# mLSTM states of a hybrid decoder step stored as 64+1 columns a head pair instead of 2 x (64+1), with the sample update's masked keys made by GpSimd

## What is computed

```
a    = einsum(q, k) * d_w                                  # scores with decay weights
num  = a @ v + inter_w * (q @ C)                           # "inter" part reads the state
den  = sum(a)  + inter_w * (q @ n)
h    = num / max(|den|, exp(-m_t))
C    = decay * C + einsum('s,sk,sv->kv', w_s, k, v)        # update
n    = decay * n + einsum('s,sk->k', w_s, k)
```

## Time and profile before

| | us |
|---|---|
| median of 3 runs (lowest to highest) | 2176.08 (2172.74 to 2176.18) |
| the profiled execution's own time | 2176.46 |
| its span on the core | 2174.6 |
| TensorE busy | 1987.2 (91%) |
| VectorE busy | 963.5 (44%) |
| ScalarE busy | 430.4 (20%) |
| GpSimd busy | 80.1 (4%) |

### The profile page before, as it was taken

How to read it: one execution, slowest core, us unless ns; L and a number is a source line. 1 busy time by engine, 2 the same in 40 slices (tenths; PEclk the granted TensorE clock), 3 DMA queues, 4 the chain that set the end, 5 groups by cost and what they waited for, 6 DMA issues and landing times.

```text
span 2174.6 us, 30150 instructions
## 1 busy us (share of the span) xinstructions
PE 1987.2 (91%) x13082; PEld 1868.7 (86%) x13082; DVE 963.5 (44%) x1661; ACT 430.4 (20%) x803; POOL 80.1 (4%) x71
## 2 busy tenths in 40 slices
PE   5998887999797698889987798999999999999997
PEld 5997657999787468878986498999999999999997
DVE  7323674565366346684233125333333333332344
ACT  2003671011220143131023302110001000000126
POOL 3000002000101200000000000000000000000000
PEclk9999999999777799999999999999999999999998
DMA  4314802110242784134130511111111111111112
GB/s 143 111 29 160 310 2 53 39 49 22 94 180 97 273 339 164 40 97 126 29 135 17 197 39 39 39 46 36 53 39 46 36 53 43 42 37 53 44 34 83
DMA packets 165878, 188.55 MB, mean 87 GB/s; under 512 B 15919, under 2 KB 153679, under 8 KB 161050
## 3 DMA queue, kind: packets, MB, share of 16 engines
q1 hardware_dynamic: 164250, 153.70, 21.7%
q10 hardware_dynamic: 1536, 33.56, 4.0%
HBM read 170.46 MB, written 50.33 MB: 102 GB/s over the span
## 4 chain that ended last, share of the span: by engine, by line
PE 82%; DVE 9%; ACT 4%; issue 2%; SPq 1%; DMA 1%; DVEq 0%; ACTq 0%
PE psum L253 64%; PE psum L2025 2%; PE psum L485 2%; PE psum L1697 1%; PE psum L1297 1%; DVE x_lo L291 1%; PE psum L1000 1%; PE psum L509 1%; SPq L1239 1%; PE psum L497 1%; PE psum L990 1%; ACT wide L579 1%; PE psum L1348 1%; ACT scratch L1718 1%; PE psum L1312 1%
## 5 line engine op out<-in xcount | busy, mean ns | idle before, releaser
L253 PE MATMUL psum<-x_lo,weights_hi 128*128 128x384 f32 (+1 forms) x2328 | 517.9, 330 | 0.0
L253 PE MATMUL psum<-x_hi,weights_hi 128*128 128x384 f32 (+1 forms) x2136 | 479.2, 332 | 34.6 <-DVE x_lo L291 24.3
L253 PE MATMUL psum<-x_hi,weights_lo 128*128 128x384 f32 (+1 forms) x2136 | 473.9, 330 | 0.0
L208 DVE CAST weights_hi<-weights_raw 128x1024 fp32r<-128x1024 f32 (+1 forms) x138 | 91.9, 666 | 731.6 <-PE psum L253 719.1
L253 PEld LDWEIGHTS psum<-x_hi,weights_hi 128*128 128x128 f32 x2136 | 368.3, 190 | 39.7 <-issue 27.1
L253 PEld LDWEIGHTS psum<-x_lo,weights_hi 128*128 128x128 f32 x2328 | 402.0, 190 | 0.0
L253 PEld LDWEIGHTS psum<-x_hi,weights_lo 128*128 128x128 f32 x2136 | 368.4, 189 | 0.0
L210 DVE TENSOR_TENSOR weights_lo<-weights_raw,weights_hi 128x1024 fp32r<-128x1024 f32 (+1 forms) x138 | 161.7, 1172 | 4.7
L1941 ACT ACTIVATE scratch<-scratch 128x1088 f32<-128x1088 f32 x22 | 24.5, 1116 | 419.9 <-DVE scratch L1955 419.9
L253 PE MATMUL psum<-hidden_hi,weights_hi 128*128 128x384 f32 (+1 forms) x432 | 95.2, 328 | 0.0
L253 PE MATMUL psum<-hidden_lo,weights_hi 128*128 128x384 f32 (+1 forms) x432 | 95.2, 328 | 0.0
(11 more groups left out here) (338 smaller groups left out, 2408.2 us busy)
## 6 DMA issues: line engine op xcount, KB each, us to landing
weights_raw<-in_w_in_dram SPq DMA_DIRECT2D x28, 512.0 KB, 3.7
work<-in_cache_win_k_dram SPq DMA_DIRECT2D x6, 2048.0 KB, 13.1
work<-in_cache_win_v_dram ACTq DMA_DIRECT2D x6, 2048.0 KB, 12.8
weights_raw<-in_w_gate_dram SPq DMA_DIRECT2D x22, 512.0 KB, 3.7
weights_raw<-in_w_up_dram SPq DMA_DIRECT2D x22, 512.0 KB, 3.7
weights_raw<-in_w_down_dram SPq DMA_DIRECT2D x24, 384.0 KB, 3.3
weights_work<-in_cache_mem_k_dram SPq DMA_DIRECT2D x8, 1024.0 KB, 5.1
work<-in_cache_mem_v_dram SPq DMA_DIRECT2D x8, 1024.0 KB, 10.7
```

The source lines that it names most:

```text
L208: nc.vector.tensor_copy(whi[:, w, 0:nk, :], raw[:, w, 0:nk, :]).then_inc(w_high, 1)
L253: mm = nc.tensor.matmul(PS[:, 3 * s + c, 0:n], w[:, slot, k0 + k], x[part][:, k0 + k, t0:t0 + n], start=(k == 0 and w is whi and part == 0 ...
```

## The change

The odd head's block moves from columns 65:130 to columns 0:65 of its rows, so a pair takes 65 columns on all 128 partitions and nothing in a state is zero padding.

- Inter products read on row groups: two products a pair, K = 64 rows each, with 65 columns moving; the even heads go to bank 6, the odd to bank 7. 8 products a chunk for 4, and 64 for 32 in the sample phase.
- Update products write on column groups: one product a head, 64 weight columns, 65 moving, to PSUM rows 0:64 or 64:128 of one bank; 8 products for 4. In the sample phase they use bank 6 or 7 and no longer bank 4, so the wait for `c_cat` goes.
- Decay is one instruction for two, the addition one for four, the n copies one for two.
- The sample states are not zeroed; the 16 loads become 8 of 128 KB without a wait, the 18 state stores become 9.
- The masked keys are made by GpSimd, after its q mask and kw of the sample chunk, instead of VectorE.

```diff
-        cst = cut(XN, ML0 + 3448, NP, 2 * V1W)
+        cst = cut(XN, ML0 + 3448, NP, V1W)
-        sample_c = cut(WRT, 0, DB, NP * 2 * V1W)
+        sample_c = cut(WRT, 0, DB, NP * V1W)
...
+        def state_update_tensor(pe, k, c, n, bank):
+            for h in range(H):
+                p, rows = h // 2, slice(HD * (h % 2), HD * (h % 2) + HD)
+                mm = nc.tensor.matmul(PS[rows, bank, p * V1W:(p + 1) * V1W], k[0:n, h * HD:(h + 1) * HD],
+                                      v1[0:n, c, h * V1W:(h + 1) * V1W], start=True, stop=True, tile_position=(0, HD * (h % 2)))
+            return mm
...
                 for p in range(NP):
-                    mm = nc.tensor.matmul(PS[:, 6 + p // 2, (p % 2) * 2 * V1W:(p % 2 + 1) * 2 * V1W], qk[:, p, c * P:(c + 1) * P],
-                                          cst[:, p, :], start=True, stop=True)
+                    for e in range(2):
+                        rows = slice(HD * e, HD * e + HD)
+                        mm = nc.tensor.matmul(PS[:, 6 + e, p * V1W:(p + 1) * V1W], qk[rows, p, c * P:(c + 1) * P],
+                                              cst[rows, p, :], start=True, stop=True, tile_position=(HD * e, 0))
...
-                for p in range(NP):
-                    mm = nc.tensor.matmul(PS[:, 6 + p // 2, (p % 2) * 2 * V1W:(p % 2 + 1) * 2 * V1W], kw[:, p * P:(p + 1) * P],
-                                          v1[:, c, p * 2 * V1W:(p + 1) * 2 * V1W], start=True, stop=True)
-                mm.then_inc(c_upd, 1)
+                state_update_tensor(pe, kw, c, P, 6).then_inc(c_upd, 1)
...
         def state_decay(state, c):
-            for e in range(2):
-                rows, cs = slice(HD * e, HD * e + HD), slice(V1W * e, V1W * e + V1W)
-                last = nc.vector.tensor_tensor(state[rows, :, cs], state[rows, :, cs],
-                                               dec[rows, :, c:c + 1].to_broadcast([HD, NP, V1W]), ALU.mult)
-            chains["dve"](last)
+            chains["dve"](nc.vector.tensor_tensor(state, state, dec[:, :, c:c + 1].to_broadcast([P, NP, V1W]), ALU.mult))
-        def state_add(state, banks, signal):
-            for e in range(2):
-                rows, cs = slice(HD * e, HD * e + HD), slice(V1W * e, V1W * e + V1W)
-                for a in range(2):
-                    upd = PS[rows, banks + a, 0:4 * V1W].rearrange("p (j d) -> p j d", j=2)
-                    last = nc.vector.tensor_tensor(state[rows, 2 * a:2 * a + 2, cs], upd[:, :, cs], state[rows, 2 * a:2 * a + 2, cs], ALU.add)
-            last.then_inc(signal, 1)
+        def state_add(state, bank, signal):
+            upd = PS[:, bank, 0:4 * V1W].rearrange("p (j d) -> p j d", j=NP)
+            nc.vector.tensor_tensor(state, upd, state, ALU.add).then_inc(signal, 1)
...
+        def masked_k_pool(pool):
+            pool.wait_ge(c_kw, NC + 1)
+            for b in range(DB):
+                if b >= 2:
+                    pool.wait_ge(su_ready, b - 1)
+                nc.gpsimd.tensor_scalar(kwm[0:NS, b % 2, :], kw[0:NS, :], batch_sel[0:NS, b:b + 1], None, ALU.mult).then_inc(kwm_ready, 1)
...
                 for b in range(DB):
-                    mm = nc.tensor.matmul(PS[0:NS, 6 + p // 2, (p % 2) * 2 * V1W:(p % 2 + 1) * 2 * V1W],
-                                          q_mask[:, b, p * NS:(p + 1) * NS], sc4[:, b, p, :], start=(b == 0), stop=(b == DB - 1))
+                    for e in range(2):
+                        rows = slice(HD * e, HD * e + HD)
+                        nc.tensor.matmul(PS[0:NS, 6 + e, p * V1W:(p + 1) * V1W], q_mask[rows, b, p * NS:(p + 1) * NS],
+                                         sc4[rows, b, p, :], start=(b == 0), stop=(b == DB - 1), tile_position=(HD * e, 0))
...
             for b in range(DB):
                 pe.wait_ge(kwm_ready, b + 1)
-                if b == 0:
-                    pe.wait_ge(c_cat, NC + 1)
                 if b >= 2:
                     pe.wait_ge(su_done, b - 1)
-                for p in range(NP):
-                    mm = nc.tensor.matmul(PS[:, bank + p // 2, (p % 2) * 2 * V1W:(p % 2 + 1) * 2 * V1W],
-                                          kwm[0:NS, b % 2, p * P:(p + 1) * P], v1[0:NS, NC, p * 2 * V1W:(p + 1) * 2 * V1W],
-                                          start=True, stop=True)
-                mm.then_inc(su_ready, 1)
+                state_update_tensor(pe, kwm[:, b % 2, :], NC, NS, 6 + b % 2).then_inc(su_ready, 1)
...
             for b in range(DB):
-                if b + 1 < DB:
-                    masked(b + 1)
                 state_decay(sc4[:, b], NC + b)
                 dve.wait_ge(su_ready, b + 1)
-                state_add(sc4[:, b], 4 + 2 * (b % 2), su_done)
+                state_add(sc4[:, b], 6 + b % 2, su_done)
...
         def state_store(sp):
-                for e in range(2):
-                    rows, c64 = slice(HD * e, HD * e + HD), slice(V1W * e, V1W * e + HD)
-                    stored(sp.dma_start(cp[e, :, 0], cst[rows, :, c64]))
-                    for b in range(DB):
-                        stored(sp.dma_start(cs[e, :, b], sc4[rows, b, :, c64]))
+                stored(sp.dma_start(cp[:, 0], cst[:, :, 0:HD]))
+                for b in range(DB):
+                    stored(sp.dma_start(cs[:, b], sc4[:, b, :, 0:HD]))
```

More of the change, by code:

```diff
@@ L1195, in sample_vector @@
             dve.wait_ge(n_turned, 1)
-            dve.wait_ge(sc_landed, 16 * 16)
-            for e in range(2):
-                rows = slice(HD * e, HD * e + HD)
-                last = nc.vector.tensor_copy(sc4[rows, :, :, V1W * e + HD], PS[rows, 7, 480:512].rearrange("p (b j) -> p b j", b=DB))
-            last.then_inc(n_put, 1)
+            dve.wait_ge(sc_landed, 16 * DB)
+            nc.vector.tensor_copy(sc4[:, :, :, HD], PS[:, 7, 480:512].rearrange("p (b j) -> p b j", b=DB)).then_inc(n_put, 1)
             chunk_logits(dve, NC, NS, sample_causal[0:NS])
@@ L1206, in sample_vector @@
             chunk_place(dve, NC, NS, SEQ)
-            dve.wait_ge(c_kw, NC + 1)
-            def masked(b):
-                if b >= 2:
-                    dve.wait_ge(su_ready, b - 1)
-                nc.vector.tensor_scalar(kwm[0:NS, b % 2, :], kw[0:NS, :], batch_sel[0:NS, b:b + 1], None, ALU.mult).then_inc(kwm_ready, 1)
-            masked(0)
             for b in range(DB):
-                if b + 1 < DB:
-                    masked(b + 1)
                 state_decay(sc4[:, b], NC + b)
                 dve.wait_ge(su_ready, b + 1)
-                state_add(sc4[:, b], 4 + 2 * (b % 2), su_done)
+                state_add(sc4[:, b], 6 + b % 2, su_done)
             dve.wait_ge(su_done, DB)
-            for e in range(2):
-                rows = slice(HD * e, HD * e + HD)
-                nc.vector.tensor_copy(n_stage[rows, 0:DB * NP].rearrange("p (b j) -> p b j", b=DB), sc4[rows, :, :, V1W * e + HD])
-                last = nc.vector.tensor_copy(n_stage[rows, DB * NP:(DB + 1) * NP], cst[rows, :, V1W * e + HD])
-            last.then_inc(n_ready, 1)
+            nc.vector.tensor_copy(n_stage[:, 0:DB * NP].rearrange("p (b j) -> p b j", b=DB), sc4[:, :, :, HD])
+            nc.vector.tensor_copy(n_stage[:, DB * NP:(DB + 1) * NP], cst[:, :, HD]).then_inc(n_ready, 1)
             dve.wait_ge(n_rows_ready, 1)
@@ L2447, in _ @@
                     chunk_pool(pool, [NC])
+                    masked_k_pool(pool)
                 elif name == "cross":
```

27 lines of the change are left out of this document (10 added, 17 removed).

## The result

The kernel after takes **2186.86 us** (median of 4 runs, 2184.51 to 2188.61), the kernel before 2174.41 (the three runs of the table above and one more): ratio 1.0054, 95% interval 1.0039 to 1.0069. It is slower, by half a per cent. The forecast was 2159.1, and the range, 2148 to 2168, does not hold the result. The profiled execution's span is 2184.5 for 2174.6 before.

The account below looks back on a forecast made before the run. Neither TensorE nor VectorE is full in the changed phases; they take turns, so each hand-over counts. -5.0 + 3.2 - 3.1 - 8.6 - 3.5 = -17.0 from 2176.46 gives 2159.5, 2159.1 against the median; range 2148 to 2168.

Parts of the forecast that it names:

- rival 3: Chunk phase: TensorE is granted less clock for narrower pieces, 0.66 instead of 0.78, costing 14.2 us; 2173.3, chance 0.08.
- an update 0.94 sooner: Chunks: the update products take 1.05 us at half clock instead of 1.99; nobody on the path waits for them.
- collision: Chunks: GpSimd's earlier kw holds up VectorE's small steps, h starts 0.8 us later in four chunks: +3.2.
- Rival 4: Chunk and sample products: the array's halves don't overlap, so doubled instructions take double time; +14.4, 2190.5, chance 0.04.
- Additions: Chunks, VectorE: four additions (1.00 us) become one of 0.38, saving 0.62 in each of 8 chunks: -5.0.
- Rival 1: GpSimd doesn't block VectorE: first, no chunk collision; second, the update loop goes by masks alone, -11.2; 2153.3, chance 0.25.
- Changes of tiling: Chunks, TensorE: 16 new changes of tiling mode might cost up to 0.10 us each, +1.6; taken as 0.
- Inter products in the chunks: Chunks, TensorE: 16 narrower instructions for 8, +2 at worst, -2 at best; taken as 0.
- Sample inter products: Sample phase, TensorE: 128 narrower instructions take 5.9 us where 64 took 9.0: -3.1.
- Update loop: Sample phase: GpSimd's mask (1.04) and VectorE's decay (0.42) exclude each other, 1.46 a stream, GpSimd the bound: -8.6.
- Stores: After the sample phase: issue sets SP's pace, so nine stores of 0.80 us become 4.5 of double size: -3.5.
- The bad end of the range: Whole kernel: all bounds on the bad side summed to -7.8, or 2168.

Follow-up runs that it names:

- e10: Kernel after, with GpSimd's kw in the chunks waiting until h is made, no added work: 2179.31 us, ratio 1.0024.
- e4: Kernel after plus 4 unread products of 128x128 weights and 130 columns behind each chunk's update: 2156.97 us, ratio 0.9925.
- e5: Kernel after plus 16 unread narrow products of the new update's shape behind each chunk's update: 2158.09 us, ratio 0.9933.
- e11: Kernel after plus e4's unread products, placed ahead of the inter products where TensorE has no gap: 2196.76 us, ratio 1.0117.
- e2: Kernel after with the chunks' inter products on the whole array again, prompt state in 130 columns: 2173.99 us, ratio 0.9998.
- e6: Kernel after with e4's unread products and the masks back on VectorE: 2154.86 us, ratio 0.9918.
- e9: e7 with its state stores in halves of 64 rows, 16 stores instead of 8: 2158.01 us, ratio 0.9928.
- e7: Kernel after with e4's unread products, masks back on VectorE and e10's wait of kw for h: 2152.24 us, ratio 0.9901.
- e3: Kernel after with the chunks' inter and update products both on the whole array again, sample phase new: 2157.93 us, ratio 0.9922.
- e13: Kernel after plus 8 of e5's 16 unread narrow products behind each chunk's update: 2181.17 us, ratio 1.0032.

## Why the prediction was wrong

**The step that failed** is the treatment of TensorE's clock. The sum costs every product of the chunk phase as if the clock of before, 0.78, stayed, and sets the clock apart in rival 3, at a chance of 0.08 and a fall to 0.66. It fell to 0.52. Rival 3's own formula gives 77.9 x (0.78 / 0.52 - 1) = 39 with that number, and 28.6 for the work that was left, as above. The evidence stood in the rows that I read: the clock was 0.57 in 690 to 720, in which products are short and separated by waits, and "an update 0.94 sooner" was booked as costing nobody but GpSimd. Its other side is more idle time on TensorE in every chunk, 0.71 as measured (0.65 before, 1.36 in e10, which has no collision), and the collision that I did forecast added 0.8 to the same gap. I priced both as delays, never as something that the clock answers to. The experiments show that it is: unread products in the gap are worth 29 us (e4, e5), as many in another place win nothing (e11). The narrower inter products lower the clock too, at an unchanged gap (0.69 in e2, 0.52 in the kernel after), and for that part the cause stays open.

**The sign.** Rival 4 was the slower case and named 2190.5, near the result, but by luck: its mechanism is refuted. The halves of the array overlap: the chunk update's 16 instructions take 1.14 at the lower level (1.05 forecast), the sample inter product's 128 take 5.3, not 12.3.

**The other terms.**

- *Additions*, -5.0: nearly right by the rows. One addition is 0.42 for 0.38 forecast, against 1.00 for the four, which makes -4.6. No run changes the additions alone.
- *Collision*, +3.2: right in kind and in size for a chunk. The small step takes 0.98, the gap is 0.81 longer than in e10, which takes GpSimd out of the way. It came in all seven chunks; in the three that paid before it replaces an h of 1.47. Rival 1's first half is refuted. The Trainium skill ("GPSIMD Engine Reference", Key points) names VectorE's instructions with two SBUF inputs and those in a perf mode that uses two ports. The two-input step here agrees. In some chunks it is a one-input step of 8 columns that is blocked (0.95 for 0.17 in e5), and no run shows in which mode it ran.
- *Changes of tiling*, 0: right as far as the trace tells. L1016 starts at 623.34, before the modelled end of L1000 (623.41).
- *Inter products in the chunks*, 0: 1.98 at the lower level, inside the bounds. The 1.83 that stood for this level is that of a product whose neighbour before it ran at the upper one; the next chunk of the kernel before has 2.10.
- *Sample inter products*, -3.1: -3.7 (5.3 for 9.0).
- *Update loop*, -8.6: -7.0. GpSimd is the bound of the loop, as said, but for another reason. The sum has 1.04 for a mask and 0.42 for a decay that excludes it. The decay doesn't, as the rows above show, and the six masks in the loop take 10.18 one behind the other, 1.70 each: the loop goes by the mask alone, as rival 1's second half has it, at a price above the 1.41 that I took for the worst. Two errors of opposite sign make the term look better than it is. The row that I took the price from has a second operand that repeats 8 columns; with a scalar from on-chip memory in its place GpSimd is slower, not faster. The Trainium skill ("GPSIMD Engine Reference", Engine selection) gives one-input operations roughly line rate. The kernel after has 1.67, against VectorE's 0.47 in e6, and the measurement decides.
- *Stores*, -3.5: about right. Halves against whole stores are 3.8 in the SP queue and 3.9 at the restart (e9, e7). Between before and after, the last store ends 3.9 sooner after the end of the phase (28.0 to 24.1), and the restart moved by 2.3 (30.6 to 28.4).

The sum without the clock was sound in size: e3, which has all of this but the chunks' products and additions, is 17.2 us below the kernel before beside it, and the forecast for those terms is 15.2. In e3's trace 3.3 of the difference lies in the chunk phase, where nothing was forecast for it, at a clock of 0.81 for 0.78. The bad end of the range left out two bounds that the text gives, 2 for the inter products and 1.6 for the changes of tiling; with them it is 2172, still far below the result.

## What to carry to other kernels

In a phase of short, dependent products at a granted clock between the two levels, don't cost an edit at the clock of before: write down where TensorE's idle time goes, chunk by chunk, and give a longer gap a price at the lower level throughout. Making a product off the critical path faster only lengthens the wait behind it. Here that took the gap from 0.65 to 1.36, and another engine's instruction let in by it from 1.36 to 2.17; with wide inter products the narrow update cost 16 us (e2 against e3), about as much as all the rest of the change won. Before such an edit is dropped, fill the gap with unread products of the size that went. Price a GpSimd operation by a row of the same kind, scalar operand included, and move work to it only where nobody waits for the result.

## What the runs showed of the hardware

- The granted clock of the chunk phase goes from 0.52 to 0.92 with 1.15 us of unread products (2.0 at the lower level) in each chunk's gap (e5). As much work elsewhere in the chunk leaves it at 0.55 (e11), and half of it at 0.60 (e13).
- GpSimd multiplies 64 x 512 by a scalar from memory in 1.55 (the first two, with VectorE mostly idle) and 1.70 in the loop, against 1.03 for a product of 64 x 512 with a second operand that repeats 8 columns, in the same phase.
- A GpSimd product of two tensors (1.04) holds up a VectorE step of 8 columns until it is over: 0.98 for 0.17 with two inputs, 0.95 with one (e5). GpSimd's product with a scalar from memory doesn't do this to VectorE's two-input decays: of the seven that start in its 10.2 us of masks, six take 0.42 and one 0.61.
